# Another order of splits, picks and row operations inside one round of an expert stage

## The reference

```python
def block(args):
    hb, eb, gb = args
    a = jnp.einsum('td,tkd->tk', hb, u_tab[eb])
    w = gb.astype(hb.dtype) * jax.nn.gelu(a, approximate=False)
    return jnp.einsum('tk,tkd->td', w, v_tab[eb])
...
x = x + mod[5] * peer(...)
```

## Time and profile before

| | us |
|---|---|
| median of 3 runs | 4223.01 (4220.87 to 4224.71) |
| span of the profiled execution | 4219.0 |
| TensorE busy | 3869.5 (92%) |
| VectorE busy | 3528.4 (84%) |
| ScalarE busy | 1945.1 (46%) |
| GpSimd busy | 1105.8 (26%) |

### The profile page before, as it was taken

The page is one execution under the profiler, slowest core; times in us unless marked ns, Lnnn a source line. Parts: engine busy times, 40 slices in busy tenths (PEclk is TensorE's granted clock), DMA queues, the critical chain, the costliest instruction groups (busy, mean ns, idle before and its releaser), DMA issues. The chain is left out here.

```text
span 4219.0 us, 69815 instructions
## 1 busy us (share of the span) xinstructions
PE 3869.5 (92%) x23631; PEld 3337.2 (79%) x23631; DVE 3528.4 (84%) x6910; ACT 1945.1 (46%) x3599; POOL 1105.8 (26%) x1095
## 2 busy tenths in 40 slices
PE   7969989988999999999999897898868999999998
PEld 6854468877888888888888776336767999999998
DVE  5387948999799999999999966666998899999998
ACT  4367532147444444444444355654246444444443
POOL 0000000039443434434334300000046333333332
PEclk9979999869999999999999998999979999999999
DMA  5102321246899999999999821112237999999997
GB/s 194 55 17 65 89 67 46 70 123 191 326 382 364 381 364 381 370 372 370 384 366 383 333 66 46 44 45 77 68 100 247 371 369 376 369 376 369 377 368 290
DMA packets 246997, 1018.18 MB, mean 241 GB/s; under 512 B 17121, under 2 KB 115521, under 8 KB 146641
## 3 DMA queue, kind: packets, MB, share of 16 engines
q0 software_dynamic: 85296, 599.59, 36.7%
q1 hardware_dynamic: 161504, 416.31, 28.2%
HBM read 963.34 MB, written 52.43 MB: 241 GB/s over the span
## 5 line engine op out<-in xcount | busy, mean ns | idle before, releaser
L1397 POOL DMA_INDIRECT rows<-rows,pick_i x512 | 790.6, 1544 | 1156.5 <-DVE y_tok L2663 653.2
L525 PE MATMUL psA<-h_hi,split_hi 128*128 128x448 f32 (+3 forms) x2768 | 971.8, 351 | 88.8 <-DVE xT L2642 54.7
L2027 DVE TENSOR_TENSOR split_lo<-raw,split_hi 128x1024 fp32r<-128x1024 f32 x596 | 727.9, 1221 | 303.2 <-ACT split_hi L1441 296.8
L525 PE MATMUL psA<-h_lo,split_hi 128*128 128x448 f32 (+3 forms) x2768 | 952.1, 344 | 0.0
L525 PE MATMUL psA<-h_hi,split_lo 128*128 128x448 f32 (+3 forms) x2768 | 951.8, 344 | 0.0
L1441 ACT ACTIVATE split_hi<-raw 128x1024 fp32r<-128x1024 f32 x596 | 628.3, 1054 | 304.2 <-DMA raw<-expert_pairs 153.4
L525 PEld LDWEIGHTS psA<-h_hi,split_hi 128*128 128x128 f32 x2768 | 527.5, 191 | 165.6 <-issue 112.8
L2651 DVE CUSTOM_DVE_ANT_1 rows<-rows,h_wide 128x1024 f32<-128x1024 f32 x512 | 624.8, 1220 | 25.5 <-DMA rows<-rows,pick_i 23.4
L2663 DVE SCALAR_TENSOR_TENSOR y_tok<-rows,pick_w,y_tok 128x1024 f32<-128x1024 f32 x444 | 569.1, 1282 | 5.9
L525 PEld LDWEIGHTS psA<-h_hi,split_lo 128*128 128x128 f32 x2768 | 527.3, 190 | 35.6
L525 PEld LDWEIGHTS psA<-h_lo,split_hi 128*128 128x128 f32 x2768 | 527.9, 191 | 33.3
(11 more groups left out here) (344 smaller groups left out, 6321.3 us busy)
## 6 DMA issues: line engine op xcount, KB each, us to landing
raw<-expert_pairs SPq DMA_DIRECT2D x256, 1024.0 KB, 7.2
gates<-g_buf SPq DMA_DIRECT2D x22, 2048.0 KB, 8.7
raw<-tiles SPq DMA_DIRECT2D x84, 512.0 KB, 3.7
raw<-mod_tiles SPq DMA_DIRECT2D x80, 512.0 KB, 3.6
g_in<-gates POOLq DMA_DIRECT2D x32, 896.0 KB, 9.0
g_in<-gates POOLq DMA_DIRECT2D x32, 640.0 KB, 5.9
mod_w<-mod_pairs SPq DMA_DIRECT2D x8, 1024.0 KB, 19.9
rows<-rows,pick_i POOLq DMA_INDIRECT x512, 8.4
```

Source lines behind the costliest of these rows:

```text
L525: ins = nc.tensor.matmul(out_, lhsT, rhs, start=start, stop=stop)
L1397: nc.gpsimd.indirect_dma_start(rows[l][:, b, :], None, (rows0, rows1)[l], bass.IndirectOffsetOnAxis(pick_i[:, u:u + 1], 0))\
L2027: V.tensor_tensor(split_lo[:, n % SPLIT].rearrange("p k n -> p (k n)"), raw[:, n % RAW, :], split_hi[:, n % SPLIT].rearrange("p k n -> p ( ...
```

## The change

Only the order inside a round is different, in ScalarE's and VectorE's program. No instruction is added or dropped, and no buffer or semaphore changes. The lists `spread` are replaced by an order written out for each layer.

In layer 0 VectorE's round was: product 0, 2 row steps, split 1, 2 row steps, product 1, split 2, 2 row steps, add of the shared chunk, split 3, low 0, 2 row steps, split 4, low 1, 2 row steps. It becomes: 2 row steps, product 0, 1 row step, split 1, 3 row steps, product 1, 1 row step, split 2, add of the shared chunk, 2 row steps, low 0, split 3, 1 row step, low 1, split 4. ScalarE's was: gelu 0, weigh, split 1, weigh, gelu 1, weigh, split 2, split 3, high 0, weigh, split 4, high 1, weigh. It becomes: gelu 0, weigh, split 1, 2 weighs, gelu 1, split 2, weigh, split 3, high 0, weigh, high 1, split 4.

In layer 1 ScalarE's order comes out as it was. VectorE's was: product 0, 1 row step, split 1, 1 row step, product 1, split 2, 1 row step, split 3, low 0, 1 row step, split 4, low 1, 2 row steps. It becomes: product 0, 1 row step, split 1, 2 row steps, product 1, split 2, split 3, low 0, 1 row step, split 4, low 1, 2 row steps. One accumulate moves from behind split 2 to the place ahead of product 1.

ScalarE:

```diff
-            spread = ((1, 1, 1, 1, 1), (0, 1, 1, 0, 1))[l]
             for s in range(NSUPER):
-                base = EX0[l] + 4 * s + 6
-                for c in range(2):
-                    if s + 1 < NSUPER:
-                        gelu(c, s + 1)
-                    weigh(spread[2 * c])
-                    split_to(min(base + c + 1, end))
-                    weigh(spread[1] if c == 0 else 0)
-                for c in range(2):
-                    split_to(min(base + c + 3, end))
-                    if s + 1 < NSUPER:
-                        high(c, s + 1)
-                    weigh(spread[3 + c])
+                base, more = EX0[l] + 4 * s + 6, s + 1 < NSUPER
+
+                def split_before(m):
+                    split_to(min(base + m, end))
+
+                if more:
+                    gelu(0, s + 1)
+                if l == 0:
+                    weigh(1)
+                    split_before(1)
+                    weigh(2)
+                    if more:
+                        gelu(1, s + 1)
+                    split_before(2)
+                    weigh(1)
+                    split_before(3)
+                    if more:
+                        high(0, s + 1)
+                    weigh(1)
+                    if more:
+                        high(1, s + 1)
+                    split_before(4)
+                else:
+                    split_before(1)
+                    weigh(1)
+                    if more:
+                        gelu(1, s + 1)
+                    weigh(1)
+                    split_before(2)
+                    split_before(3)
+                    if more:
+                        high(0, s + 1)
+                    split_before(4)
+                    if more:
+                        high(1, s + 1)
+                    weigh(1)
```

VectorE:

```diff
-            spread = ((2, 2, 2, 2, 2), (1, 1, 1, 1, 2))[l]
             for s in range(NSUPER):
-                base = EX0[l] + 4 * s + 6
-                if s + 1 < NSUPER:
-                    product(0, s + 1)
-                row_work(spread[0])
-                split_to(min(base + 1, end))
-                row_work(spread[1])
-                if s + 1 < NSUPER:
-                    product(1, s + 1)
-                split_to(min(base + 2, end))
-                row_work(spread[2])
-                if CYCLED[l] is not None:
+                base, more = EX0[l] + 4 * s + 6, s + 1 < NSUPER
+
+                def split_before(m):
+                    split_to(min(base + m, end))
+
+                if l == 0:
+                    row_work(2)
+                    if more:
+                        product(0, s + 1)
+                    row_work(1)
+                    split_before(1)
+                    row_work(3)
+                    if more:
+                        product(1, s + 1)
+                    row_work(1)
+                    split_before(2)
                     dve.wait_ge(cycled_full, seen.upto(cycled_full))
                     add_chunk(psA[:, 0, 0:n], CYCLED[l], 0, n).then_inc(cycled_free, 1)
-                for c in range(2):
-                    split_to(min(base + c + 3, end))
-                    if s + 1 < NSUPER:
-                        low(c, s + 1)
-                    row_work(spread[3 + c])
+                    row_work(2)
+                    if more:
+                        low(0, s + 1)
+                    split_before(3)
+                    row_work(1)
+                    if more:
+                        low(1, s + 1)
+                    split_before(4)
+                else:
+                    if more:
+                        product(0, s + 1)
+                    row_work(1)
+                    split_before(1)
+                    row_work(2)
+                    if more:
+                        product(1, s + 1)
+                    split_before(2)
+                    split_before(3)
+                    if more:
+                        low(0, s + 1)
+                    row_work(1)
+                    split_before(4)
+                    if more:
+                        low(1, s + 1)
+                    row_work(2)
```

## The result

The changed kernel takes 4118.44 us (median of 4116.35 to 4120.73), against 4223.7 before (a fourth run has joined the three of the table above): a ratio of 0.9755 with a 95% interval of 0.9741 to 0.9769, 105 us less. The profiled span goes from 4219.0 to 4116.3. The forecast was 4141, between 4110 and 4190.

The account below looks back on a forecast made before the run. Bound by the loop of VectorE's and TensorE's waits in layer 0, VectorE's pace in layer 1. Over 62 rounds, 60 us and 22 us off the 4219.0 span give 4137, plus 4 for the median: 4141 us, range 4110 to 4190.

Parts of the forecast that it names:

- The loop: Layer 0: VectorE waits 1.08 us for ScalarE's split, comes late to the add, and TensorE waits 0.92 us for it.
- The list from the add: Layer 0: VectorE's new order timed step by step from the add at 17.4 us; next add 19.54 later, no engine waiting.
- late rows: Layer 0: gathered rows that VectorE waits for, 0.21 us a round, kept in the sum and rounded up to 19.9 us.
- narrowest gather window: Layer 0: shortest time for a gathered row to land, said to widen from some 10.6 to 11.3 us.
- Layer 1: Moved accumulate fills VectorE's 1.21 us hole; round falls from 14.95 to 14.6 us, bounds 14.4 and 14.95, gaining 22 us.
- One of the prediction's signs: Sign of being right: VectorE's wait for ScalarE's split gone in both stages.
- the tight loop: Layer 1: split 2, its pair's landing, ScalarE's rounding, split 1, dot, accumulate, product: 14.3 us, just inside 14.6.
- The DMA rivals: DMA bounds layer 0 at today's packet times (4184 us, 0.18), or nothing exceeds 374 GB/s (4223 us, 0.08).
- The slower rival: Layer 0: split 1 waits for its raw pair if landings exceed 10.9 us; 4271 us at 13 us landings; chance 0.08.
- The add ahead of the chunk: Layer 0: VectorE reaches the add before the chunk is there, costing only its lead, inside 19.9 us; no separate chance.

Follow-up runs that it names:

- e5: Kernel before, with one accumulate in layer 0 moved from behind split 2 to ahead of it: 4150.29 us against 4213.93, ratio 0.9847.
- e10: Kernel before, with ScalarE's pick between gelu 1 and split 2 moved behind split 2 in layer 0: 4148.11 us against 4218.23, ratio 0.9832.
- e6: Changed kernel with ScalarE's old order put back, VectorE's new order kept: 4117.79 us against 4216.69 for the kernel before, ratio 0.9765.
- e3: Kernel before, with only the add of the shared chunk in layer 0 moved directly behind split 2: 4226.57 us against 4213.93, ratio 1.003.
- e4: Changed kernel with layer 0's add put back behind two row steps: 4118.39 us against 4216.69 for the kernel before, ratio 0.9769.
- e2: Kernel before, with the new order in layer 1 alone: 4191.02 us, ratio 0.9942, 22.9 us less.
- e1: Kernel before, with the new orders in layer 0 alone: 4143.43 us against 4213.93, ratio 0.9831.
- e8: Changed kernel with 16 of 96 matmuls a round dropped and VectorE's accumulates halved in layer 0: 4059.28 us against 4216.69 for the kernel before, ratio 0.9635.
- e9: Kernel before, with ScalarE's new order alone in layer 0 and VectorE's old one: 4445.55 us against 4218.23, ratio 1.0538.

## Why the prediction was right, and where it was off

**The loop.** That VectorE's hole and TensorE's wait are one loop held: e5 closes the hole with an accumulate ahead of split 2, as the prediction had it, e10 from ScalarE's side, each with no other change, and both waits go together. The prediction named two reasons for the hole to go, that accumulate and ScalarE's last pick behind split 2; e5 and e6 show the first to be enough, e10 the second. The add's move, in e3 and e4, is worth nothing. TensorE's wait for the add was where the loss showed, not where it arose.

**The list from the add.** The add was put at 17.4 us behind U0; it stands at 17.41. Split 2 was put at 16.0, wanted from ScalarE by then and ready near 14.2; in the round above VectorE starts it at 16.02 behind U0 and ScalarE has it at 13.97. Product 1 was put at 14.2; it is at 14.28. The start-to-start costs of the earlier trace rows are good to a tenth over a whole round. TensorE's need was put at 19.6 and the round is 19.62 to 19.64.

**The step that was mis-sized: late rows.** The sum kept's 0.21 us a round for rows that come late on top of TensorE's 19.6 and rounded up by 0.09, giving 19.9. Measured: no such wait, 19.64, and the difference of 0.26 over 62 rounds is the 16 us by which layer 0's gain of 60 fell short of 76. The prediction worked out in its next paragraph that the narrowest gather window gets wider (10.6 to 11.3 us), and didn't take that into the sum. Landings of rows after, in the tile view of the changed kernel, against the earlier trace rows:

```profile
DMA to landing us min/median/max: 6.8/9.2/12.2
```

The median got 0.7 us longer while the wait went to zero, so it isn't faster transfers. Across the kernels VectorE's wait for rows goes with the spacing of the row steps: 12.1 us (10 times) before, 13.1 (12) in e3, 7.6 (5) in e2's layer 0, 5.0 (7) in e5 and 6.1 (7) in e10, all with the old spacing or one step moved; none in the changed kernel and e4, 0.4 and 0.6 (once each) in e1 and e6, all with the new. That the width of the narrowest window is the cause is argued from this; no run varied a window alone.

**Layer 1.** 14.6 was taken between bounds of 14.4 and 14.95; 14.51 came, 0.09 x 62 = 5 us more than the 22. That VectorE's hole in front of split 2 was what held TensorE back proved right. In the changed kernel VectorE's timeline, which answers the earlier trace rows, has no hole of that size left in front of splits 2 and 3, and TensorE's around the starts of V0a and of U1 shows the plain spacing of 0.14 to 0.15 that the earlier trace rows lacked:

```profile
3606.31 1.28 DVE L2686 SCALAR_TENSOR_TENSOR y_tok<-rows,pick_w,y_tok 128x1024 f32<-128x1024 f32 x1
3607.51 0.48 DVE L2655 TENSOR_TENSOR gel<-gel,g_in 128x320 f32<-128x320 f32 x1
3608.01 2.48 DVE L2050 TENSOR_TENSOR split_lo<-raw,split_hi 128x1024 fp32r<-128x1024 f32 x2
```

```profile
3613.71 0.31 PE L525 MATMUL psA<-h_hi,split_lo 128*128 128x320 f32 x1
3613.85 0.31 PE L525 MATMUL psV<-W_hi,split_hi 128*128 128x320 f32 x1
...
3615.47 0.31 PE L525 MATMUL psV<-W_hi,split_lo 128*128 128x320 f32 x1
3615.61 0.31 PE L525 MATMUL psA<-h_hi,split_hi 128*128 128x320 f32 x1
3615.76 0.30 PE L525 MATMUL psA<-h_lo,split_hi 128*128 128x320 f32 x1
```

The prediction had worked out 14.68 with the delay at U1 alone and 14.4 with the same again at V0a, and took a time between them without V0a's own spacing in the sum. Its rows in the kernel before, one round's start of V0a in TensorE's timeline:

```profile
3504.85 0.31 PE L525 MATMUL psA<-h_hi,split_lo 128*128 128x320 f32 x1
3505.06 0.42 PE L525 MATMUL psV<-W_hi,split_hi 128*128 128x320 f32 x1
3505.32 0.31 PE L525 MATMUL psV<-W_lo,split_hi 128*128 128x320 f32 x1
```

V0a comes 0.21 behind U0's last matmul and its second 0.26 behind its first, in place of 0.15 each: 0.17 us. With U1's 0.27 that is 0.44, and 14.95 - 0.44 = 14.51, the time that came. It is not the luck of one round: over the 53 rounds between 3300 and 4100 us the same four spacings exceed the plain ones by 0.44 in the mean, and none of them does after. The term was in the trace to be read, and the earlier trace rows had it too: TensorE's matmul row showed 799.51 of 800 us, but its weight loads (PEld) 777.35, and 699.98 of 700 after. The 22.65 us that they stood idle are 0.42 us a round. (In layer 0 the weight loads fill only 92% even after, so this reading works in layer 1 alone.)

One of the prediction's signs failed here. VectorE's wait for ScalarE's split was to be gone in both stages, and in layer 1 it isn't. Between 3250 and 4000 us:

```profile
ACT split_hi L1441 <- DMA raw<-expert_pairs: 137.4, 53, 4.2
...
DVE split_lo L2050 <- ACT split_hi L1441: 32.3, 51, 1.5
```

It stands elsewhere now: in front of split 2 there is hardly any left, but split 1 waits in about half of the rounds and split 4 in a third. In the round behind the one shown, split 1 starts at 3619.29, 1.52 us late, because ScalarE had waited 3.60 us for its raw pair. So the tight loop that the prediction put at 14.3 us, just inside the round, does bind now and then, and a wait of that size at split 1 was its sign of being wrong. It is 0.6 us in the mean of a round in which VectorE has some 0.8 to spare (14.51 less 13.7), and TensorE's row is full, so it costs nothing; the margin is small.

**The DMA rivals.** 392 GB/s were asked for at 19.9 us; 398 came at 19.64, and 415 in e8. A bound at 374 GB/s, or at a busy share of 1.0 with today's packets (20.24 us a round), is refuted by the round of 19.64. The Trainium skill's limit of about 358 GB/s for a core ("DMA: Bandwidth & Descriptors", section "Where 436 GB/s comes from") does not hold here. Another page of the Trainium skill, "HBM Reference", section "Specifications (TRN2)", says that a core which streams alone measures near 425 and that the 358 are its share when both cores of a pair stream. This kernel runs on one core, and the 415 of e8, near that figure and beneath it, agree.

**The slower rival.** Raw pairs do come closer to late in layer 0: ScalarE's split waits for raw 40 times, 39.9 us. The landings stayed at 6.3/8.1/10.7 us, where the price began at 10.9 and a loss at 11.9 in the mean. VectorE, two us behind ScalarE at split 2, waits for a split once, 0.2 us.

**The add ahead of the chunk.** This rival came true and cost no more than VectorE's lead, as the prediction said: VectorE waits for the chunk 37 times, 8.3 us in all, while TensorE is busy throughout.

**The remaining 2 us.** The median lay 4 us above the span before and 2 above it after. So 16 + 5 + 2 makes up the 23 us between 4141 and 4118.

## What to carry to other kernels

When two engines each have a small hole in every round, follow the chain through both queues before choosing which to mend: here one in-order chain (dot, pick, rounding, split) made both, and one step moved on either engine closed both, while the move that faced the visible wait did nothing. Read two in-order queues as a pair, and check every place where one waits for the other: ScalarE's half of this change alone cost 5%, VectorE's half alone brought all of the gain. And when the working says that a wait should shrink, let the sum follow it, or say why not.

## What was not expected of the hardware

A DMA busy share near 1 was no ceiling. In layer 0 the share went 0.97, 0.99, 1.01 while the rate went 374, 398, 415 GB/s: 4% more busy time, 11% more bytes. The busy time per byte fell by 6%, so in the kernel before some of what counted as busy was packets that took longer than they needed to.

A wait on TensorE can be followed by slower matmuls. In the round of e9 shown below TensorE waits 2.36 us for gelu 1, and then, from 1522.35 to 1525.34, its matmuls start 0.37 us apart instead of 0.2055. Windows of e9, all engines, columns as in the earlier trace rows, and the matmul that ends the wait:

```profile
1510.00:1517.00 7.00, 6.85 (x34) 6.32 (x35) 6.96 (x10) 1.73 (x5) 2.83 (x2) 1.00 0.94 335
1521.40:1526.00 4.60, 4.60 (x15) 4.11 (x16) 4.17 (x6) 0.87 (x1) 0.81 (x1) 0.63 1.02 423
1527.00:1531.00 4.00, 4.00 (x20) 3.65 (x20) 3.21 (x4) 1.21 (x2) 0.00 (x0) 1.00 0.98 373
```

```profile
1521.37 0.47 PE L525 MATMUL psA<-W_hi,split_hi 128*128 128x448 f32 x1 [2.36 <-ACT gel L1939]
```

The granted clock is 0.63 in the mean of the middle window; in windows of one us inside it, from 1522.4 to 1525.4, it is 0.50, the lower of its two levels (1.2 of 2.4 GHz), with full speed before and after. It is not what made e9 slow: the add at 1525.98 waited for VectorE's dot, with the chunk done at 1523.1. Over the stretch from 1150 to 2250 us the clock is 0.96 in e9 and 0.98 to 1.00 in every other kernel of the study.
